# Layer 1's attention: products with V one tile behind, turned maps in two places, next scores biased first

## The chip, the cores and the metric

The kernel runs on one core of one Trainium2 chip. The metric is the device time of one execution in microseconds; given is the median of several runs. The engines are called as in the profile: PE (TensorE), DVE (VectorE), ACT (ScalarE), POOL (GpSimd), SP (SyncE); PEld are TensorE's weight loads.

## What is computed

A decoder trunk of two layers over 1024 tokens of 1024 channels, in float32. Layer 0 has a differential attention and a pooling mixer, layer 1 a gated short convolution and a dilated attention; each is followed by an output projection and a SwiGLU FFN. The change touches layer 1's attention alone, in the reference:

```
for layer in range(DEPTH):
    h = rmsnorm(x, norm_mix[layer])
    ...
        yc = short_conv_gate(bg, cg, hc, od_conv_w[i])
        q = rmsnorm(q.reshape(bsz, seq, D_HEADS, HEAD_DIM), od_q_gain[i])
        k = rmsnorm(k.reshape(bsz, seq, D_HEADS, HEAD_DIM), od_k_gain[i])
        v = v.reshape(bsz, seq, D_HEADS, HEAD_DIM)
        yd = dilated_attention(q, k, v, slopes_d).reshape(bsz, seq, D_WIDTH)
        x = x + jnp.concatenate([yc, yd], axis=-1) @ od_w_out[i]
    x = x + swiglu_ffn(x, norm_ffn[layer], ...)
```

There are 8 heads of 64 channels. The three branches of the dilated attention (a near window, every 4th and every 16th key) come to one softmax over the causal keys, in which a key counts as many times as branches hold it: the kernel adds one table of distances times the head's slope and of logarithms of that count to the scores.

## The kernel before, in words

The kernel is written out by hand, one instruction stream for each engine, with semaphores between them. Every engine runs its own list in order; nothing reorders the work.

**Tiles and units.** Layer 1's attention has 4 units (UNITS) of two heads each, m = 0 and 1, and in each unit 8 tiles (NT) of 128 queries, i = 0 to 7, so 32 tiles n = 8u + i (TILES0). Tile i has 128(i + 1) causal keys. Per tile and head the steps are:
- score (L973): two products of 512 columns at most for each half of the keys, with K1 and K2, into banks 0-1 (m = 0) or 2-3 (m = 1) of PS. It is made two tiles ahead of the rest, and waits (s_mx) for the bias of the tile before, which empties the bank.
- bias (biased, L2058, on DVE): scores plus the table, into PR[m][i % 2], with the row's extreme into NMX.
- expo (L1529, ACT): the exponential in place, with its row sum into DEN.
- turn (L985, PE): i + 1 transposes of PR into one of three banks of PS (4 to 6), taken in turn by turn_bank (L391); for i >= 4 it fills a second bank (c = 1). It waits for expo and for the copy that empties its bank.
- turned: ACT (L1547) copies up to 512 columns to PT[m], DVE (L2170) the columns above 512.
- weigh (L1005, PE): the product of the turned map PT[m] with V, 2(i + 1) PE instructions of 64 columns, into bank 7 (weighed, L394), which both heads share. So it waits for o_ok of the other head, that is, for the scaled output that empties the bank.
- scaled (L2176, DVE): reciprocal of DEN (L2180), then the output times it into Y (L2182).

**Order on TensorE (L1178 to L1199)**, per tile: turn 0, score 0 of tile i + 2, turn 1, weigh 0, score 1 of tile i + 2, weigh 1. **On VectorE (L2167 to L2207)**, per tile: biased 0 of tile i + 1, at i = 6 the next unit's table for head 0 (next_bias, L2051), scaled 1 of tile i - 1, turned 0, biased 1 of tile i + 1, turned 1, scaled 0; at i = 6 the next unit's table for head 1; at i = 7 scaled 1 as well. **On ScalarE (L1636 to L1658)**, per tile: turned 0, expo 0 of the next tile, turned 1, expo 1 of the next tile.

**The next unit's stacks.** Queries and keys of the next unit are split into a high part (ACT, stack_high L1498) and the rest (POOL, low_stack L841, its instruction at L845) while the unit runs: six pieces in a fixed order (STACK, L353), keys 0 and 1, then queries in four pieces. In layer 1 ACT makes pieces 0 and 1 at tiles 1 and 2, piece 2 ahead of turned 0 of tile 6, piece 3 after expo 0 there, piece 4 after expo 1 there, and piece 5 after turned 1 of tile 7. The queries go to the same QST that the unit reads, so they can't be made before its scores are done. PE waits for pieces 2 and 3 ahead of the scores of tile 6, and at the first tile of a unit, ahead of turn 0, for all six:

```
if i == 0:
    pe.wait_ge(stack_lo, following)
```

After the last tile PE turns Y (turn_y, L1132) and begins the output projection, whose weights ACT and DVE split after the last product (L1660, L2210).

Of the kernel before, what the change touches and what calls it, by code (L numbers as in the profile page):

```python
# [82 lines left out]
def trunk(nc, a, out):  # L83
    ctx = ExitStack()
    with ctx:
# [152 lines left out]
        PR = [[at(f"PR{m}{b}", [P, TOK], F32, oHL + 16 * KB + 8 * KB * m + 4 * KB * b) for b in range(2)] for m in range(2)]  # L238
        YJ = at("YJ", [P, P], F32, oK + 4 * KB)
# [684 lines left out]
        def _(pe):  # L924
# [60 lines left out]
            def turn(L, m, g, h, i):  # L985

                if L == 0:
                    if g + i > 0:
                        pe.wait_ge(t_ea[0][0], g + i)
                    pe.wait_ge(c_ok, g + i + 1)  # L990
                else:
                    pe.wait_ge(s_ex[m][L], g + i + 1)
                for c in range(i // 4 + 1):
                    if L == 1 and TURNS.index((m, i, c)) >= 3:
                        m0, i0, c0 = TURNS[TURNS.index((m, i, c)) - 3]
                        if c0 == 0:
                            pe.wait_ge(t_ea[m0][1], g + i0 + 1)
                        else:
                            pe.wait_ge(t_ed[m0][1], h + i0 - 3)
                    for j in range(4 * c, min(4 * c + 4, i + 1)):  # L1000
                        last = pe.transpose(turn_bank(L, m, i, c)[:, P * (j - 4 * c):P * (j - 4 * c) + P],  # L1001
                                            PR[m if L else 1][i % 2][:, P * j:P * j + P], IDN[:])
                last.then_inc(t_pe[m][L], 1)

            def weigh(L, m, u, g, h, i):  # L1005

                pe.wait_ge(t_ea[m][L], g + i + 1)
                if L == 1 and i >= 4:
                    pe.wait_ge(t_ed[m][1], h + i - 3)

                if L == 0:
                    pe.wait_ge(o_ok[0][0], g + i + 2)
                else:
                    pe.wait_ge(o_ok[1 - m][1], g + i + 2 + m)
                w, off = (P, u * P) if L == 0 else (HD, u * P + HD * m)
                for j in range(i + 1):
                    last = pe.matmul(weighed(L, m, i), PT[m if L else i % 2][:, P * j:P * j + P], V[:, j, bass.ds(off, w)],  # L1017
# [12 lines left out]
            for L in range(2):  # L1030
# [117 lines left out]
                if L == 0:  # L1148
                    for u in range(UNITS):
                        b, g = u % 2, NT * u  # L1150
                        following = stacks_before(0, u + 1)
                        for i in range(NT):
# [11 lines left out]
                            if i > 0:  # L1164
                                weigh(0, 0, u, g, 0, i - 1)
                            elif u > 0:
                                weigh(0, 0, u - 1, g - NT, 0, NT - 1)
# [4 lines left out]
                            turn(0, 0, g, 0, i)  # L1172
# [3 lines left out]
                    weigh(0, 0, UNITS - 1, NT * (UNITS - 1), 0, NT - 1)  # L1176
                else:
                    for u in range(UNITS):  # L1178
                        b, g, h = u % 2, NT * u, 4 * u
                        following = stacks_before(1, u + 1)  # L1180
                        for i in range(NT):
# [5 lines left out]
                            turn(1, 0, g, h, i)  # L1187
# [5 lines left out]
                            turn(1, 1, g, h, i)  # L1193
                            weigh(1, 0, u, g, h, i)
# [4 lines left out]
                            weigh(1, 1, u, g, h, i)  # L1199
# [165 lines left out]
        def _(act):  # L1365
# [73 lines left out]
            for L in range(2):  # L1439
# [107 lines left out]
                def turned(m, g, i):  # L1547
# [6 lines left out]
                    else:  # L1554
                        w = min(HALF, P * (i + 1))
                        src, to = turn_bank(1, m, i, 0)[:, 0:w], PT[m]
# [285 lines left out]
        def _(dve):  # L1842
# [93 lines left out]
            for L in range(2):  # L1936
# [229 lines left out]
                else:  # L2166
                    for u in range(UNITS):  # L2167
                        b, g = u % 2, NT * u

                        def turned(m, i):  # L2170
                            if i >= 4:
                                dve.wait_ge(t_pe[m][L], g + i + 3)
                                w = P * (i + 1)
                                v.tensor_copy(PT[m][:, HALF:w], turn_bank(1, m, i, 1)[:, 0:w - HALF]).then_inc(t_ed[m][1], 1)

                        def scaled(m, i):  # L2176

                            c = m + 2 * (i % 2)
                            dve.wait_ge(s_ex[m][1], g + i + 1)
                            att.link(v.reciprocal(RDN[:, c:c + 1], DEN[:, c:c + 1]))  # L2180
                            dve.wait_ge(o_pe[m][1], g + i + 1)
                            v.tensor_scalar(Y[:, i, bass.ds(u * P + HD * m, HD)], weighed(1, m, i), RDN[:, c:c + 1], None,  # L2182
                                            ALU.mult).then_inc(o_ok[m][1], 1)
# [5 lines left out]
                        for i in range(NT):  # L2189
                            if i == NT - 1:  # L2190
                                att.wait()
                            more = u + 1 < UNITS or i + 1 < NT
                            if more:
                                biased(0, b, g, i + 1)
                            if i == NT - 2 and u + 1 < UNITS:
                                next_bias(0)
                            if i > 0:
# [274 lines left out]
```

## Time and profile before

| | us |
|---|---|
| median of 3 runs | 2240.63 (2240.45 to 2242.11) |
| the profiled execution, its own time | 2241.53 |
| its span in the profile | 2239.7 |
| PE busy | 2183.4 (97%) |
| DVE busy | 1256.6 (56%) |
| ACT busy | 878.5 (39%) |
| POOL busy | 790.5 (35%) |
| layer 1's attention in that span | 1350 to 1497 |

Times in rows are microseconds from the start of the span; a row of a timeline gives start, duration, engine, line, operation, output<-inputs, shape and count, and in brackets the engine's idle time before it with what ended it. Starts are recorded and ends of matmuls are modelled, so matmuls that follow each other overlap in the rows, and an idle time is shorter than the gap from start to start. PEclk is the granted TensorE clock as a share of 2.4 GHz.

### The profile page before, as it was taken

Reading aid. Unit: us, or ns where it says so; the run is one execution under the profiler, and the core shown is the slowest. Engines: PE = TensorE matmul, PEld = TensorE weight load, DVE = VectorE, ACT = ScalarE, POOL = GpSimd, SP = SyncE. Lnnn points to the kernel's source line nnn. Section 1 sums busy time; section 2 is a strip of 40 time slices with the busy share of each in tenths; the row PEclk is TensorE's granted clock in tenths of the full one; section 3 lists DMA queues with packets and bytes.
Section 4 is the critical chain, followed back from the end, with each engine's and each line's share of the span. In section 5 each row is a group of like instructions: output and inputs, shape, how many; then the busy total and the mean of one; then the engine's idle time right before and its main releaser. Section 6 shows DMA issues by size and latency. Waiting matters only on the chain.

```text
span 2239.7 us, 29918 instructions
## 1 busy us (share of the span) xinstructions
PE 2183.4 (97%) x10632; PEld 1827.2 (82%) x10632; DVE 1256.6 (56%) x1761; ACT 878.5 (39%) x1433; POOL 790.5 (35%) x533
## 2 busy tenths in 40 slices
PE   8999899999999999999999998999999999999999
PEld 7886798888888887888888877888888888887887
DVE  4245875775555654557322246665775555554555
ACT  4124874443333334444211137652443333334433
POOL 1022542467676662002000032200467676662000
PEclk9999999999999999999999999999999999999999
DMA  5021120055555547674111111101055555547665
GB/s 182 10 78 30 39 86 20 19 179 197 197 188 169 165 158 264 192 242 124 38 45 49 47 57 38 39 20 57 21 177 197 197 188 169 169 161 262 196 190 196
DMA packets 218908, 282.92 MB, mean 126 GB/s; under 512 B 11441, under 2 KB 120497, under 8 KB 218801
## 3 DMA queue, kind: packets, MB, share of 16 engines
q1 hardware_dynamic: 218512, 281.45, 39.1%
q8 instruction: 66, 1.08, 0.2%
q14 instruction: 42, 0.34, 0.1%
q10 hardware_dynamic: 288, 0.05, 0.0%
HBM read 199.67 MB, written 73.40 MB: 122 GB/s over the span
## 4 chain that ended last, share of the span: by engine, by line
PE 72%; issue 12%; DVE 3%; ACT 2%; POOL 1%; DMA 0%; SPq 0%; POOLq 0%; DVEq 0%; ACTq 0%
PE PS L1312 12%; PE PS L1314 12%; PE PS L1313 12%; PE PS L1339 6%; PE PS L1340 6%; PE PS L1341 6%; PE PS L1017 4%; PE PS L927 2%; PE PS L929 2%; PE PS L928 2%; PE PS L1001 2%; PE PS L981 1%; PE PS L982 1%; PE PS L945 1%; POOL QRS L838 1%
## 5 line engine op out<-in xcount | busy, mean ns | idle before, releaser
L1848 DVE TENSOR_TENSOR LINEl<-LINE,HIGH 128x1024 fp32r<-128x1024 f32 x154 | 193.8, 1264 | 170.3 <-ACT HIGH L1370 170.0
L1370 ACT ACTIVATE HIGH<-LINE 128x1024 fp32r<-128x1024 f32 x154 | 162.5, 1059 | 236.7 <-PE PS L1341 234.2
L1339 PE MATMUL PS<-HIGH 128*128 128x512 f32 x616 | 241.4, 392 | 7.0 <-DVE LINEl L1848 7.0
L1340 PE MATMUL PS<-LINEl,HIGH 128*128 128x512 f32 x616 | 241.1, 391 | 0.0
L1341 PE MATMUL PS<-HIGH,LINEl 128*128 128x512 f32 x616 | 241.0, 391 | 0.0
L1848 DVE TENSOR_TENSOR SLOTl<-BLOCKS,RING 128x512 fp32r<-128x512 f32 x168 | 155.1, 923 | 96.6 <-ACT RING L1370 92.1
L807 POOL TENSOR_TENSOR ST<-ST 128x512 f32<-128x512 f32 x132 | 194.5, 1474 | 34.6 <-DMA ST<-in_ffn_w_down 26.0
L1370 ACT ACTIVATE RING<-BLOCKS 128x512 fp32r<-128x512 f32 x168 | 105.9, 631 | 227.7 <-PE PS L1314 219.4
L1848 DVE TENSOR_TENSOR SLOTl<-SLOT,RING 128x512 fp32r<-128x512 f32 x126 | 137.2, 1089 | 85.9 <-ACT RING L1370 85.7
L838 POOL TENSOR_TENSOR QRS<-QMS,EXPO 128x8 f32<-128x8 f32 x32 | 52.0, 1639 | 375.4 <-DVE QMS L2016 375.3
L1339 PEld LDWEIGHTS PS<-HIGH 128*128 128x128 f32 x616 | 116.5, 189 | 32.6 <-DVE LINEl L1848 8.3
L1341 PEld LDWEIGHTS PS<-HIGH,LINEl 128*128 128x128 f32 x616 | 116.5, 189 | 24.2
L1340 PEld LDWEIGHTS PS<-LINEl,HIGH 128*128 128x128 f32 x616 | 116.2, 189 | 24.1
L1312 PE MATMUL PS<-B1h,RING 128*128 128x512 f32 x336 | 130.7, 389 | 0.0
L1313 PE MATMUL PS<-B1l,RING 128*128 128x512 f32 x336 | 130.7, 389 | 0.0
L1314 PE MATMUL PS<-B1h,SLOTl 128*128 128x512 f32 x336 | 130.7, 389 | 0.0
L1370 ACT ACTIVATE RING<-SLOT 128x512 fp32r<-128x512 f32 x126 | 79.2, 630 | 125.2 <-PE PS L1314 114.9
L1017 PE MATMUL PS<-V,PT 128*128 128x64 f32 (+1 forms) x864 | 112.8, 276 | 10.4 <-ACT Y L1370 7.9
L1017 PEld LDWEIGHTS PS<-V,PT 128*128 128x128 f32 x864 | 106.3, 193 | 18.7 <-ACT PT L1370 12.3
L779 POOL TENSOR_TENSOR SLOT<-BLOCKS 128x512 f32<-128x512 f32 x42 | 55.3, 1317 | 187.7 <-DMA BLOCKS<-in_ffn_w_up 187.7
L812 POOL TENSOR_TENSOR RST<-MSQ,EXPO 128x1 f32<-128x1 f32 x32 | 22.9, 718 | 265.8 <-DVE MSQ L1866 265.8
L2069 DVE CUSTOM_DVE_ANT_0 PR<-PS,BIAS 128x256 f32<-128x256 f32 (+7 forms) x128 | 96.3, 755 | 18.9 <-PE PS L1001 8.7
(304 smaller groups left out, 5662.2 us busy)
## 6 DMA issues: line engine op xcount, KB each, us to landing
LINE<-hidden SPq DMA_DIRECT2D x154, 256.0 KB, 2.8
hidden<-HID SPq DMA_DIRECT2D x44, 512.0 KB, 4.5
ST<-in_ffn_w_down SPq DMA_DIRECT2D x44, 512.0 KB, 4.1
sums<-ST SPq DMA_DIRECT2D x22, 1024.0 KB, 6.2
hidden<-ST SPq DMA_DIRECT2D x22, 1024.0 KB, 6.8
LINE<-sums SPq DMA_DIRECT2D x88, 256.0 KB, 3.0
BLOCKS<-in_ffn_w_gate SPq DMA_DIRECT2D x42, 512.0 KB, 4.0
BLOCKS<-in_ffn_w_up SPq DMA_DIRECT2D x42, 512.0 KB, 5.2
```

Of the source, the lines that this page charges most:

```text
L807: nc.gpsimd.tensor_tensor(dst, x, y, op).then_inc(st_sum, 1)
L838: nc.gpsimd.tensor_tensor(QRS[:, 8 * b:8 * b + 8], QMS[:, 8 * b:8 * b + 8], EXPO[:, 0:8], ALU.pow).then_inc(qk_rs, 1)
L1017: last = pe.matmul(weighed(L, m, i), PT[m if L else i % 2][:, P * j:P * j + P], V[:, j, bass.ds(off, w)], start=(j == 0), stop=(j == i))
L1312: pe.matmul(dst, lh, rh[:, k, :], start=k == 0 and not adds_on, stop=False, skip_group_check=adds_on)
L1313: pe.matmul(dst, lh, rl[:, k, :], start=False, stop=False, skip_group_check=adds_on)
L1314: last = pe.matmul(dst, ll, rh[:, k, :], start=False, stop=k == 3, skip_group_check=adds_on)
L1339: pe.matmul(dst, hi[:, 0, ts], hi[:, 1, :], start=j == 0 and not adds_on, stop=False, skip_group_check=adds_on)
L1340: pe.matmul(dst, hi[:, 0, ts], lo[:, 1, :], start=False, stop=False, skip_group_check=adds_on)
L1341: pe.matmul(dst, lo[:, 0, ts], hi[:, 1, :], start=False, stop=j == NJ - 1, skip_group_check=adds_on).then_inc(dn_pe, 1)
L1370: return nc.scalar.activation(dst, src, ACT.Copy, **kw)
L1848: return v.tensor_tensor(dst, src, hi.bitcast(F32), ALU.subtract)
L2069: v.tensor_tensor_reduce(out=PR[m][t % 2][:, 0:keys], in0=PS[:, 1024 * m:1024 * m + keys], in1=table, scale=-1.0, scalar=3.0e38, op0=ALU.a ...
```

## The change

It concerns layer 1's attention, on three engines.
- Storage: a second place for the turned map of each head, PTL[m][1], over the keys' and queries' first rows of QK (unit 0's), free once unit 0's stacks are made. ACT and DVE wait for that (stack_lo) and for the product of two tiles ago (o_pe), in the place of waits that the single buffer did not need.
- PE: per tile turn 0, score 0 of tile i + 2, weigh 0 of the tile before, turn 1, score 1 of tile i + 2, weigh 1 of the tile before; the two products of the last tile stand behind the loop. The bank waits of turn now run on across units.
- DVE: per tile the reciprocal of head 0 of the tile before, biased 0 of the next tile, the reciprocal of head 1, scaled 1 of two tiles ago, biased 1, turned 0, (tile 6: next unit's table for head 0), scaled 0 of the tile before, turned 1, (tile 6: next table for head 1).
- ACT: the place it writes to, and the wait for it. Its order, POOL's and SP's lists are unchanged. Layer 0's calls are rewritten for the new arguments and do the same.

```diff
@@ -236,6 +236,8 @@
         BIAS = [at(f"BIAS{m}", [P, TOK], F32, oHL + 4 * KB * m) for m in range(2)]
         PT = [at(f"PT{m}", [P, TOK], F32, oHL + 8 * KB + 4 * KB * m) for m in range(2)]
         PR = [[at(f"PR{m}{b}", [P, TOK], F32, oHL + 16 * KB + 8 * KB * m + 4 * KB * b) for b in range(2)] for m in range(2)]
+
+        PTL = [[PT[m], at(f"PTB{m}", [P, TOK], F32, oC + 16 * KB * m)] for m in range(2)]
         YJ = at("YJ", [P, P], F32, oK + 4 * KB)
 
         SM = small("SM", 16 + 64)
@@ -982,39 +984,42 @@
                     last = pe.matmul(dst, q, K2[b][m][:, c0:c1], start=False, stop=True)
                 last.then_inc(s_pe[m][L], 1)
 
-            def turn(L, m, g, h, i):
-
+            def turn(L, m, u, i):
+                n = NT * u + i
                 if L == 0:
-                    if g + i > 0:
-                        pe.wait_ge(t_ea[0][0], g + i)
-                    pe.wait_ge(c_ok, g + i + 1)
+                    if n > 0:
+                        pe.wait_ge(t_ea[0][0], n)
+                    pe.wait_ge(c_ok, n + 1)
                 else:
-                    pe.wait_ge(s_ex[m][L], g + i + 1)
+                    pe.wait_ge(s_ex[m][L], n + 1)
                 for c in range(i // 4 + 1):
-                    if L == 1 and TURNS.index((m, i, c)) >= 3:
-                        m0, i0, c0 = TURNS[TURNS.index((m, i, c)) - 3]
+                    if L == 1 and (u > 0 or TURNS.index((m, i, c)) >= 3):
+
+                        u0, k0 = divmod(len(TURNS) * u + TURNS.index((m, i, c)) - 3, len(TURNS))
+                        m0, i0, c0 = TURNS[k0]
                         if c0 == 0:
-                            pe.wait_ge(t_ea[m0][1], g + i0 + 1)
+                            pe.wait_ge(t_ea[m0][1], NT * u0 + i0 + 1)
                         else:
-                            pe.wait_ge(t_ed[m0][1], h + i0 - 3)
+                            pe.wait_ge(t_ed[m0][1], 4 * u0 + i0 - 3)
                     for j in range(4 * c, min(4 * c + 4, i + 1)):
                         last = pe.transpose(turn_bank(L, m, i, c)[:, P * (j - 4 * c):P * (j - 4 * c) + P],
                                             PR[m if L else 1][i % 2][:, P * j:P * j + P], IDN[:])
                 last.then_inc(t_pe[m][L], 1)
 
-            def weigh(L, m, u, g, h, i):
-
-                pe.wait_ge(t_ea[m][L], g + i + 1)
+            def weigh(L, m, n):
+
+                u, i = n // NT, n % NT
+                pe.wait_ge(t_ea[m][L], n + 1)
                 if L == 1 and i >= 4:
-                    pe.wait_ge(t_ed[m][1], h + i - 3)
-
+                    pe.wait_ge(t_ed[m][1], 4 * u + i - 3)
                 if L == 0:
-                    pe.wait_ge(o_ok[0][0], g + i + 2)
+                    pe.wait_ge(o_ok[0][0], n + 2)
                 else:
-                    pe.wait_ge(o_ok[1 - m][1], g + i + 2 + m)
+                    pe.wait_ge(o_ok[1 - m][1], n + 2 + m)
                 w, off = (P, u * P) if L == 0 else (HD, u * P + HD * m)
+                turned = PTL[m][i % 2] if L else PT[i % 2]
                 for j in range(i + 1):
-                    last = pe.matmul(weighed(L, m, i), PT[m if L else i % 2][:, P * j:P * j + P], V[:, j, bass.ds(off, w)],
+                    last = pe.matmul(weighed(L, m, i), turned[:, P * j:P * j + P], V[:, j, off:off + w],
                                      start=(j == 0), stop=(j == i))
                 last.then_inc(o_pe[m][L], 1)
 
...
@@ -1184,19 +1187,24 @@
                                 pe.wait_ge(stack_lo, following)
                             if i == 2 and u == 0:
                                 pe.wait_ge(staged_rest, 128)
-                            turn(1, 0, g, h, i)
+                            turn(1, 0, u, i)
                             if i == NT - 2 and more:
                                 pe.wait_ge(staged[1 - b], 128 + 64 * (u // 2 + b + 1))
                                 pe.wait_ge(stack_lo, following + 3)
                             if more:
                                 score(1, 0, b, g, i + 2)
-                            turn(1, 1, g, h, i)
-                            weigh(1, 0, u, g, h, i)
+
+                            if g + i > 0:
+                                weigh(1, 0, g + i - 1)
+                            turn(1, 1, u, i)
                             if i == NT - 2 and more:
                                 pe.wait_ge(stack_lo, following + 4)
                             if more:
                                 score(1, 1, b, g, i + 2)
-                            weigh(1, 1, u, g, h, i)
+                            if g + i > 0:
+                                weigh(1, 1, g + i - 1)
+                    for m in range(2):
+                        weigh(1, m, TILES0 - 1)
 
                 if L == 0:
                     for k in range(BLOCKS_IN, 4 * NT):
@@ -1553,7 +1561,11 @@
                         src, to = PS[:, 4 * HALF:4 * HALF + w], PT[i % 2]
                     else:
                         w = min(HALF, P * (i + 1))
-                        src, to = turn_bank(1, m, i, 0)[:, 0:w], PT[m]
+                        if g + i >= 2:
+                            act.wait_ge(o_pe[m][1], g + i - 1)
+                        elif i == 1:
+                            act.wait_ge(stack_lo, STACK_AT[1] + len(STACK0))
+                        src, to = turn_bank(1, m, i, 0)[:, 0:w], PTL[m][i % 2]
                     copy(to[:, 0:w], src).then_inc(t_ea[m][L], 1)
 
                 def scaled(n):
@@ -2164,48 +2176,61 @@
                             unit_scaled(u - 1)
                     add_block(BLOCKS_IN - 1)
                 else:
-                    for u in range(UNITS):
-                        b, g = u % 2, NT * u
-
-                        def turned(m, i):
-                            if i >= 4:
-                                dve.wait_ge(t_pe[m][L], g + i + 3)
-                                w = P * (i + 1)
-                                v.tensor_copy(PT[m][:, HALF:w], turn_bank(1, m, i, 1)[:, 0:w - HALF]).then_inc(t_ed[m][1], 1)
-
-                        def scaled(m, i):
-
-                            c = m + 2 * (i % 2)
-                            dve.wait_ge(s_ex[m][1], g + i + 1)
-                            att.link(v.reciprocal(RDN[:, c:c + 1], DEN[:, c:c + 1]))
-                            dve.wait_ge(o_pe[m][1], g + i + 1)
-                            v.tensor_scalar(Y[:, i, bass.ds(u * P + HD * m, HD)], weighed(1, m, i), RDN[:, c:c + 1], None,
-                                            ALU.mult).then_inc(o_ok[m][1], 1)
+                    def turned(m, n):
+                        u, i = n // NT, n % NT
+                        if i >= 4:
+                            dve.wait_ge(t_pe[m][1], n + 3)
+                            dve.wait_ge(o_pe[m][1], n - 1)
+                            dve.wait_ge(stack_lo, STACK_AT[1] + len(STACK0))
+                            w = P * (i + 1)
+                            v.tensor_copy(PTL[m][i % 2][:, HALF:w], turn_bank(1, m, i, 1)[:, 0:w - HALF]).then_inc(t_ed[m][1], 1)
+
+                    def denominator(m, n):
+                        c = m + 2 * (n % 2)
+                        dve.wait_ge(s_ex[m][1], n + 1)
+                        att.did(v.reciprocal(RDN[:, c:c + 1], DEN[:, c:c + 1]))
+
+                    def scaled(m, n):
+                        u, i = n // NT, n % NT
+                        c, off = m + 2 * (n % 2), u * P + HD * m
+                        att.wait()
+                        dve.wait_ge(o_pe[m][1], n + 1)
+                        v.tensor_scalar(Y[:, i, off:off + HD], weighed(1, m, i), RDN[:, c:c + 1], None, ALU.mult).then_inc(o_ok[m][1], 1)
+
+                    for n in range(TILES0):
+                        u, i = n // NT, n % NT
+                        b, g, more = u % 2, NT * u, n + 1 < TILES0
 
                         def next_bias(m):
                             dve.wait_ge(s_mx[m][1], g + 9)
                             bias(m, 1 - b, 2 * u + 2 + m)
 
-                        for i in range(NT):
-                            if i == NT - 1:
-                                att.wait()
-                            more = u + 1 < UNITS or i + 1 < NT
-                            if more:
-                                biased(0, b, g, i + 1)
-                            if i == NT - 2 and u + 1 < UNITS:
-                                next_bias(0)
-                            if i > 0:
-                                scaled(1, i - 1)
-                            turned(0, i)
-                            if more:
-                                biased(1, b, g, i + 1)
-                            turned(1, i)
-                            scaled(0, i)
-                            if i == NT - 2 and u + 1 < UNITS:
-                                next_bias(1)
-                            if i == NT - 1:
-                                scaled(1, i)
-
+
+                        if n > 0:
+                            denominator(0, n - 1)
+                        if i == NT - 1:
+                            att.wait()
+                        if more:
+                            biased(0, b, g, i + 1)
+                        if n > 0:
+                            denominator(1, n - 1)
+                        if n > 1:
+                            scaled(1, n - 2)
+                        if more:
+                            biased(1, b, g, i + 1)
+                        turned(0, n)
+                        if i == NT - 2 and u + 1 < UNITS:
+                            next_bias(0)
+                        if n > 0:
+                            scaled(0, n - 1)
+                        turned(1, n)
+                        if i == NT - 2 and u + 1 < UNITS:
+                            next_bias(1)
+                    denominator(0, TILES0 - 1)
+                    scaled(1, TILES0 - 2)
+                    scaled(0, TILES0 - 1)
+                    denominator(1, TILES0 - 1)
+                    scaled(1, TILES0 - 1)
 
                 def split_o(g):
                     dve.wait_ge(wo_hi, WO_AT[1] + g + 1)
```

## Rows read from the trace of the kernel before

**Rows 1.** Busy time by stretch, second unit: us, PE, PEld, DVE, ACT, POOL busy, PEclk, DMA

```profile
1389.40:1425.00 35.60, 34.11 (x267) 31.29 (x266) 23.12 (x74) 24.52 (x54) 9.83 (x6) 1.00 0.13 31
```

**Rows 2.** PE's waits in the attention: us in total, times, longest

```profile
PE PS L981 <- DVE NMX L2069: 2.1, 3, 0.7
PE PS L1017 <- DVE Y L2182: 1.8, 5, 0.5
```

**Rows 3.** Timeline of PE, second unit's tiles 6 and 7, next unit's tile 0

```profile
1412.78 0.94 PE L1001 MATMUL PS<-IDN,PR 128*128 128x128 f32 x7
...
1413.73 1.23 PE L1001 MATMUL PS<-IDN,PR 128*128 128x128 f32 x7
1414.79 1.67 PE L1017 MATMUL PS<-V,PT 128*128 128x64 f32 x14
1416.77 0.33 PE L981 MATMUL PS<-K,QST 128*128 128x128 f32 x1 [0.30 <-POOL QST L845]
...
1419.73 1.26 PE L1001 MATMUL PS<-IDN,PR 128*128 128x128 f32 x8
1420.83 1.90 PE L1017 MATMUL PS<-V,PT 128*128 128x64 f32 x16
...
1422.73 0.28 PE L982 MATMUL PS<-K,QST 128*128 128x256 f32 x1
1423.26 1.97 PE L1017 MATMUL PS<-V,PT 128*128 128x64 f32 x16 [0.25 <-DVE Y L2182]
1425.07 0.28 PE L1001 MATMUL PS<-IDN,PR 128*128 128x128 f32 x1
1426.06 0.44 PE L981 MATMUL PS<-K,QST 128*128 128x384 f32 x1 [0.71 <-DVE NMX L2069]
...
1427.02 0.33 PE L982 MATMUL PS<-K,QST 128*128 128x384 f32 x1
1427.51 0.41 PE L1017 MATMUL PS<-V,PT 128*128 128x64 f32 x2
```

**Rows 4.** Timeline of ACT, same stretch

```profile
1413.75 0.60 ACT L1370 ACTIVATE PT<-PS 128x512 f32<-128x512 f32 x1 [2.41 <-PE PS L1001]
...
1421.03 0.60 ACT L1370 ACTIVATE PT<-PS 128x512 f32<-128x512 f32 x1 [0.36 <-PE PS L1001]
1421.65 0.84 ACT L1370 ACTIVATE QST<-QK 64x768 fp32r<-64x768 f32 x1
```

**Rows 5.** Timeline of POOL, same stretch

```profile
1415.99 0.72 POOL L845 TENSOR_TENSOR QST<-QK,QST 64x256 fp32r<-64x256 f32 x1 [3.84 <-ACT QST L1370]
...
1422.57 1.81 POOL L845 TENSOR_TENSOR QST<-QK,QST 64x768 fp32r<-64x768 f32 x1 [2.14 <-ACT QST L1370]
```

**Rows 6.** Timeline of DVE, same unit

```profile
1408.17 1.08 DVE L2069 CUSTOM_DVE_ANT_0 PR<-PS,BIAS 128x896 f32<-128x896 f32 x1
...
1416.78 1.28 DVE L2051 SCALAR_TENSOR_TENSOR BIAS<-DIST,SM,MASK 128x1024 f32<-128x1024 f32 x1
...
1422.84 0.28 DVE L2182 TENSOR_SCALAR Y<-PS,RDN 128x64 f32<-128x64 f32 x1 [1.05 <-PE PS L1017]
...
1425.35 0.28 DVE L2182 TENSOR_SCALAR Y<-PS,RDN 128x64 f32<-128x64 f32 x1 [2.16 <-PE PS L1017]
```

**Rows 7.** Timeline of PE, end of the last unit

```profile
1485.99 1.67 PE L1017 MATMUL PS<-V,PT 128*128 128x64 f32 x14
1488.21 1.75 PE L1017 MATMUL PS<-V,PT 128*128 128x64 f32 x14 [0.55 <-DVE Y L2182]
...
1496.97 3.60 PE L1145 MATMUL PS<-IDN,Y 128*128 128x128 f32 x16 [0.54 <-DVE Y L2182]
```

**Rows 8.** Busy time and granted clock by stretch, columns as in rows 1

```profile
1492.00:1496.50 4.50, 3.88 (x34) 3.64 (x32) 1.12 (x4) 2.49 (x3) 0.00 (x0) 1.00 0.00 0
1496.50:1501.00 4.50, 3.60 (x16) 3.27 (x16) 4.46 (x4) 3.33 (x3) 0.00 (x0) 0.62 0.01 2
1421.00:1425.00 4.00, 3.75 (x34) 3.58 (x34) 1.11 (x4) 1.93 (x4) 1.81 (x1) 1.00 0.02 4
```

More of the change, by code:

```diff
@@ L1162, in _ @@
                                 score(0, 0, b, g, i + 2)
-                            if i > 0:
-                                weigh(0, 0, u, g, 0, i - 1)
-                            elif u > 0:
-                                weigh(0, 0, u - 1, g - NT, 0, NT - 1)
+                            if g + i > 0:
+                                weigh(0, 0, g + i - 1)
                             if more:
@@ L1171, in _ @@
                                 turn_y(0)
-                            turn(0, 0, g, 0, i)
+                            turn(0, 0, u, i)
                             if g + i >= FILL_FROM:
@@ L1175, in _ @@
                     turn_y(1)
-                    weigh(0, 0, UNITS - 1, NT * (UNITS - 1), 0, NT - 1)
+                    weigh(0, 0, TILES0 - 1)
                 else:
                     for u in range(UNITS):
-                        b, g, h = u % 2, NT * u, 4 * u
+                        b, g = u % 2, NT * u
                         following = stacks_before(1, u + 1)
@@ L1198, in _ @@
                                 score(1, 1, b, g, i + 2)
-                            weigh(1, 1, u, g, h, i)
+                            if g + i > 0:
+                                weigh(1, 1, g + i - 1)
+                    for m in range(2):
+                        weigh(1, m, TILES0 - 1)
                 if L == 0:
@@ L2187, in next_bias @@
                             bias(m, 1 - b, 2 * u + 2 + m)
-                        for i in range(NT):
-                            if i == NT - 1:
-                                att.wait()
-                            more = u + 1 < UNITS or i + 1 < NT
-                            if more:
-                                biased(0, b, g, i + 1)
-                            if i == NT - 2 and u + 1 < UNITS:
-                                next_bias(0)
-                            if i > 0:
-                                scaled(1, i - 1)
-                            turned(0, i)
-                            if more:
-                                biased(1, b, g, i + 1)
-                            turned(1, i)
-                            scaled(0, i)
-                            if i == NT - 2 and u + 1 < UNITS:
-                                next_bias(1)
-                            if i == NT - 1:
-                                scaled(1, i)
+                        if n > 0:
[23 more added lines that the diff above has]
+                    scaled(1, TILES0 - 1)
                 def split_o(g):
```

## The prediction

> **What bounds it now.** I read the kernel by stretch first, then the waits, then TensorE's timeline, then what ACT, POOL and VectorE do around each wait. In layer 1's attention one unit of two heads takes 35.6 us and PE is busy 34.1 of them [rows 1]: TensorE is the bound, and only the time between its instructions can be won. The list of waits shows 2.1 us for VectorE's score maxima and 1.8 for scaled outputs [rows 2]; GpSimd's query stack comes next. Since the ends of matmuls are modelled, a wait shows whole only from start to start. In a full stream a product with V starts every 0.11 us (16 in 1.81 us, from 1423.26 to 1425.07), and a transpose too (7 in 0.69, less an overlap of 0.08 with the score behind) [rows 3]. What lies above that at tiles 6, 7, 0 and 1 of a unit:
> - the second map's turn at tile 6 takes 1.06 us for 0.77, at tile 7 1.10 for 0.88: it waits for ACT's copy, for its bank; 0.29 and 0.22 lost
> - second score at tile 6, behind GpSimd: 1.98 us after the start of 14 products worth 1.56; 0.42, with its restart 0.5
> - second product at tile 7: 0.53 us after a score half worth 0.12; 0.41 lost
> - first score at tile 0: 0.99 after one transpose of 0.11; 0.88. VectorE scales the last output (1425.35) [rows 6] before it biases the next scores, which this one waits for
> - second product at tile 0: 0.49 behind a half worth 0.18; 0.31. Tile 1 has the same wait, with a score longer by 0.12 ahead of it: 0.2.
>
> In the last unit these waits are longer, as no score lies between. From 1485.99 to 1496.97, 10.98 us, it makes 60 products (6.7) and 16 transposes (1.75) [rows 7]: 2.5 lost, of which the last 0.7, ahead of layer 1's output turns, stays; with tile 6's bank wait just before it (estimate 0.4, as tile 7's), 2.2 can go. All this is some 10 us of 2240: that is the ceiling.
>
> **The change, part by part.** No instruction of work is added or taken away; a few waits on semaphores, copies into a second place and the order change. Per tile TensorE now does turn 0, score 0, product 0 of the tile before, turn 1, score 1, product 1 of the tile before.
>
> *Waits that go.* At three unit starts: 0.88 (the bias now stands ahead of the scaled output on VectorE), 0.31 and 0.2, so 1.4 x 3 = 4.2. A product of a whole tile now lies between the two turns, so the bank waits go, and turn 1 and score 1 lie between the two products, some 1.1 us at tile 7, so that wait goes: (0.29 + 0.22 + 0.41) x 3 = 2.8. Unit 0's start runs at the half clock and gives away four products there: 0.5. In the last unit the 2.2 us go. Gone in all: 9.7.
>
> *Waits that come.* The two products still share one bank, so each waits for the scaled output of the other. Product end to VectorE's start is 0.28 us (1425.07 to 1425.35) [rows 3, 6]; from that start to the next product 0.42 (1422.84 to 1423.26) [rows 3, 6]: 0.70 in all. At tile 0 turn and score are 0.11 + 0.38 = 0.49 us, so the second product is 0.2 late, x3 = 0.6. At tile 2 VectorE has its two biases, two reciprocals and two outputs within about 2 us of TensorE's work at tile 1; bounds 0 and 0.3, I take 0.15 (what a full VectorE leaves over), x4 = 0.6. In the last unit the two products of tile 31 have nothing between: 0.7 x 2 = 1.4.
>
> *The query stacks of the next unit* are the main term. ACT copies piece 5 after its copy of the second turned map of tile 7, GpSimd then makes the low part, and TensorE's first turn of the next unit waits for that. From the end of turn 1 (1420.83) ACT starts 0.20 later, the stack copy at 1421.65 (0.84 us), GpSimd at 1422.57 for 1.81: ready at 1424.43 with 0.05 of release, 3.60 after the turn [rows 3 to 5]. Now it is covered by 4.24 us of TensorE (1420.83 to 1425.07) [rows 3]. After the change product 0 stands ahead of turn 1, so behind it only score 1 (0.25) and the product of tile 6 (14 x 0.112 = 1.56) are left: 1.81 of cover for 3.60. New wait 1.8 us at each of three unit starts: 5.4. Piece 3 at tile 6 has the same shape: ACT's chain starts at the end of turn 0 (copy 1413.75, exponential, stack copy, GpSimd 1415.99 for 0.72) [rows 4, 5] and frees score 1 at 3.99 us into the tile, as now (1412.78 to 1416.77) [rows 3]. TensorE is there at 3.1 (0.69 + 0.26 + 12 x 0.112 + 0.77), since its product is shorter and the bank wait gone: 0.9 to 1.0 lost in place of 0.5, +0.5 x 3 = 1.5. The next unit's bias (1.28 us, 1416.78) [rows 6] now stands ahead of a scaled output at tile 6; this output would be free for its product at 3.8 us, the stack frees the score at 4.0 and its two halves end at 4.3: nothing, while the stack is late; without that cover 0.4 x 3.
>
> Come in all: 0.6 + 0.6 + 1.4 + 5.4 + 1.5 = 9.5. Against 9.7, the order alone is worth -0.2 us. ACT has copies, exponentials and a key stack at tile 1, more than TensorE's new 1.8 us there (2 x (0.22 + 0.48 + 0.22)), but enters that tile early, since tile 0 now takes 4.5 with the products of tile 7: nothing.
>
> **The clock.** From 1492.0 to 1496.5 TensorE ran at the full 2.4 GHz with 34 instructions, almost all V products; in the next 4.5 us the mean is 0.62, that is 3.4 us at the half level of 1.2 GHz, and 16 transposes take 3.6 us, about 0.22 each [rows 7, 8]. What it did before the fall: V products, with idle times of 0.54 us [rows 7]. Between 1421 and 1425 V products with one wait of 0.25 kept the full clock [rows 3, 8]. A unit start with 1.8 us of idle between 14 products and 16 is emptier than the stretch before that fall. So I expect a fall at most of the three. In 3.4 us at 0.22 instead of 0.11 some 15 instructions are lost, 1.7 us; bounds 0 and 1.7, I take 1.5 as small waits run within it: 4.5.
>
> The Trainium skill (TensorE: Matmul & The Clock Gate, "Why this matters for your kernels") has the clock stay up unless PE idles for a long gap between bursts of matmuls. By that rule waits of this length cost no clock and the sum stays at -0.2; the fall after idle times of 0.54 [rows 7, 8] speaks against it.
>
> **Sum.** The profiled execution took 2241.5; 2241.5 - 0.2 + 4.5 = 2245.8; the median of the runs is 0.9 lower: 2244.9. A measurement of this kernel tells about 0.2% (4.5 us) from no change; the forecast lies inside, at the upper edge.
>
> **Rivals.**
> 1. The clock holds at the unit starts, the products on both sides of the wait being enough for it. For: the stretch at 1421 held with a small wait [rows 8]. 2241.5 - 0.2 - 0.9 = 2240.4. Chance 0.2. The rule of the Trainium skill above would give the same.
> 2. The stack is not the bound at unit starts: ACT or GpSimd would have to be 1.8 us earlier. For: GpSimd is idle 2.1 us before this piece [rows 5]. Against: that idle time is ACT's, and ACT's is TensorE's own turn [rows 4]. Then 5.4 go, 0.2 at tile 0 comes back three times, and the clock holds: 2240.4 - 5.4 + 0.6 = 2235.6, faster. Chance 0.08.
> 3. Slower. VectorE becomes late: an output of head 0 now stands behind the other head's bias and the copy of the turned map. At tile 5 this is 0.28 (latency) + 0.28 (the other output) + 1.08 (bias of 896 columns) [rows 6] + 0.4 at most for a copy of 256 columns (estimate from that row) = 2.0 us into the tile, while the product it serves ends at 0.66 + 0.94 + 10 x 0.112 = 2.7 (score of 1024 keys estimated as four halves, each 0.18 x 512/384), so 0.7 is spare. It decides once bias and copy together exceed TensorE's turn, score and product; if every tile from 2 to 5 then waits 0.2, that is 16 x 0.2 = 3.2: 2248.1. Chance 0.17.
> That two buffers free nothing, since the outputs still share a bank, is part of the sum: the last unit's 0.7.
>
> **Chances.** Forecast with falls at two or three starts: 0.55, of which 0.33 stays within 0.2% (three full falls of 1.7 reach 2245.5). With the cases above: faster 0.08, same 0.53, slower 0.39. Low end: no falls, tile 2 free: 2239.8. High end between the forecast and rival 3: 2247.5. Its own range is 2243 to 2246.
>
> **What would show it.** Right: TensorE's waits list GpSimd's query stack with 5 to 7 us in six waits (recorded idle is less than from start to start), the longest some 1.6, three of them before the first transpose of a unit; the wait for maxima at unit starts gone; bank waits gone; mean clock of the attention below before's, with two or three falls to half; the units after the first 37 us, last unit shorter. Wrong: POOL before the first turn with under 1 us (the chain), full clock throughout (the clock term), or new waits for scaled outputs at tiles 2 to 5 (rival 3).

## The result, and the profile after

The changed kernel takes 2250.1 us (median of 8 runs, 2245.4 to 2256.7) where the kernel before took 2241.0 (8 runs, 2240.4 to 2242.9): ratio 1.0036, with a 95% interval from 1.0026 to 1.0047. It is slower by 9.1 us, and it scatters over 11 us where the kernel before scatters over 2.5. The profiled execution is the slowest of the eight: 2256.7 us, span 2254.6. So its rows show more loss than the median has.

The list of TensorE's waits of the changed kernel, over layer 1's attention (in total, times, longest; PTB in the rows is the second place for a turned map):

```profile
PE PS L1005 <- POOL QST L847: 5.0, 3, 1.7
PE PS L983 <- POOL QST L847: 1.4, 3, 0.5
PE PS L1022 <- DVE Y L2198: 1.1, 2, 0.5
...
PE PS L1150 <- DVE Y L2198: 0.5, 1, 0.5
```

The waits for the maxima and for ACT's copies of [rows 2, 3] are gone, those for scaled outputs are left in the last unit alone. In their place stands the query stack: three times ahead of a unit's first turn (L1005), three times ahead of the second score of tile 6 (L983). TensorE's timeline of the changed kernel at the first unit's end, as [rows 3] one unit later (start, duration):

```profile
1372.53 0.94 PE L1005 MATMUL PS<-IDN,PR 128*128 128x128 f32 x7
...
1375.16 0.93 PE L1005 MATMUL PS<-IDN,PR 128*128 128x128 f32 x7
1376.57 0.33 PE L983 MATMUL PS<-K,QST 128*128 128x128 f32 x1 [0.47 <-POOL QST L847]
...
1379.30 1.67 PE L1022 MATMUL PS<-V,PT 128*128 128x64 f32 x14
1380.80 1.05 PE L1005 MATMUL PS<-IDN,PR 128*128 128x128 f32 x8
...
1381.92 1.67 PE L1022 MATMUL PS<-V,PT 128*128 128x64 f32 x14
1385.28 0.33 PE L1005 MATMUL PS<-IDN,PR 128*128 128x128 f32 x1 [1.68 <-POOL QST L847]
1385.36 0.42 PE L983 MATMUL PS<-K,QST 128*128 128x384 f32 x1
...
1385.80 3.35 PE L1022 MATMUL PS<-V,PTB 128*128 128x64 f32 x16
1388.94 0.42 PE L1005 MATMUL PS<-IDN,PR 128*128 128x128 f32 x1
```

and ACT's and GpSimd's share of the chain:

```profile
1381.88 0.60 ACT L1378 ACTIVATE PTB<-PS 128x512 f32<-128x512 f32 x1 [1.65 <-PE PS L1005]
1382.51 0.84 ACT L1378 ACTIVATE QST<-QK 64x768 fp32r<-64x768 f32 x1
```

```profile
1383.42 1.80 POOL L847 TENSOR_TENSOR QST<-QK,QST 64x768 fp32r<-64x768 f32 x1 [2.80 <-ACT QST L1378]
```

From the end of turn 1 (8 transposes from 1380.80, so 1381.68) to the next unit's first turn (1385.28) are 3.60 us, as foretold. 14 products from 1381.92 should have ended at 1383.48: 1.8 us lost. The second score of tile 6 starts at 4.04 us into the tile (3.99 foretold), 0.64 us behind the end of its transposes (1375.16 + 0.77), where the sum has 0.9 to 1.0. The rest of that term stands at the first score, for which the sum has none: it starts 1.05 us into the tile (1372.53 to 1373.58) where it started at 0.69, and 0.10 behind the end of GpSimd's part of piece 2 (1372.75 + 0.73).

The 16 products of tile 7 behind the wait then take 3.14 us (1385.80 to 1388.94) where they took 1.81. Busy time and granted clock of the changed kernel behind each unit's start, and at the end (us, PE, PEld, DVE, ACT, POOL busy, PEclk, DMA share, GB/s):

```profile
1384.00:1399.00 15.00, 13.72 (x72) 13.01 (x73) 5.06 (x23) 6.11 (x18) 2.82 (x2) 0.66 0.00 1
1424.00:1439.00 15.00, 13.92 (x74) 13.09 (x75) 4.99 (x23) 6.51 (x18) 3.39 (x2) 0.66 0.00 1
1460.00:1478.00 18.00, 16.32 (x85) 15.44 (x85) 5.76 (x25) 6.07 (x18) 2.00 (x2) 0.62 0.00 1
1500.00:1520.00 20.00, 17.45 (x87) 15.57 (x86) 9.83 (x14) 9.31 (x9) 0.00 (x0) 0.66 0.15 52
```

A mean of 0.66 over 15 us is 10.2 us at the half level of 1.2 GHz, 0.62 over 18 is 13.7, 0.66 over 20 is 13.6: 48 us in four falls in this slowest execution, where [rows 8] had one of 3.4. Behind the first start the clock still stands at full level for some 0.7 us: it falls at about 1385.95, TensorE having started again at 1385.28. The last fall comes between the products of tile 31, where three waits of 0.54 us follow each other:

```profile
1503.05 1.97 PE L1022 MATMUL PS<-V,PTB 128*128 128x64 f32 x16 [0.54 <-DVE Y L2198]
1505.56 3.65 PE L1022 MATMUL PS<-V,PTB 128*128 128x64 f32 x16 [0.54 <-DVE Y L2198]
1509.74 3.65 PE L1150 MATMUL PS<-IDN,Y 128*128 128x128 f32 x16 [0.54 <-DVE Y L2198]
```

It reaches into the output projection, whose products then start 0.43 us apart (0.23 in the kernel before, from 1502.32 on):

```profile
1514.32 0.77 PE L929 MATMUL PS<-WOh,HH 128*128 128x512 f32 x1 [0.93 <-DVE WOl L1860]
1514.88 0.63 PE L930 MATMUL PS<-WOl,HH 128*128 128x512 f32 x1
1515.31 0.63 PE L931 MATMUL PS<-WOh,HL 128*128 128x512 f32 x1
```

The scatter of the runs is the clock's too: those with a mean granted clock of 0.989 took 2245.4, 2246.2 and 2247.2 us, those of 0.985 took 2252.1 and 2256.7.

### The profile page after: what moved, and what is told of

Read it like the earlier page. It is cut to its first block, busy times and chain, and to the rows that moved or that the text cites. A ratio compares the mean times of both kernels' runs of the same rounds, so it can differ in the third digit from the quotient of the medians.

```text
span 2254.6 us, 30018 instructions
## 1 busy us (share of the span) xinstructions
PE 2194.7 (97%) x10632; PEld 1840.8 (82%) x10632; DVE 1257.0 (56%) x1761; ACT 879.3 (39%) x1433; POOL 791.3 (35%) x533
## 4 chain that ended last, share of the span: by engine, by line
PE 73%; issue 19%; DVE 3%; ACT 2%; POOL 2%; DMA 1%; SPq 0%; POOLq 0%; DVEq 0%; ACTq 0%
PE PS L1320 12%; PE PS L1322 12%; PE PS L1321 12%; PE PS L1347 6%; PE PS L1349 6%; PE PS L1348 6%; PE PS L1022 4%; PE PS L929 3%; PE PS L931 3%; PE PS L930 3%; PE PS L1005 2%; PE PS L983 1%; POOL QRS L840 1%; PE PS L984 1%; PE PS L947 1%
## 5 line engine op out<-in xcount | busy, mean ns | idle before, releaser
L929 PE MATMUL PS<-HH,WGh 128*128 128x512 f32 x256 | 99.8, 390 | 2.2 <-ACT V L1378 2.2
L929 PE MATMUL PS<-WQh,HH 128*128 128x512 f32 x256 | 101.8, 398 | 0.0
```

Of the source, the lines that this page charges most:

```text
L929: pe.matmul(dst, lh, rh, start=first, stop=False)
```

## Experiments

Theory A: the late piece of the query stack makes TensorE wait, and the clock falls behind that wait; both together are the loss. Its rivals: the new order on TensorE (B), the new order on VectorE (C), or the wait without the clock. Each run was timed beside the kernel before on the same chip, 2241.6 to 2242.8 us there. The changed kernel itself was timed beside 2241.0 alone, so where two runs from different chips are compared, up to 1.8 us can be the chips'; beside its own neighbour the changed kernel is at +9.1 us.

**1. Piece 5 early.** Piece 5 needs only that the unit's scores are done, which they are at tile 6:

```diff
+                        if i == NT - 1:
+                            following(5)
                         turned(0, g, i)
...
                         turned(1, g, i)
-                        if i == NT - 1:
-                            following(5)
```

> The changed kernel with one step moved: ACT makes the next unit's query piece 5 ahead of its first copy of tile 7 instead of after its second. Theory A (the late piece makes TensorE wait 1.85 us at each of three unit starts, and the clock falls there): the three waits ahead of the first turn of a unit go, no stretch at half clock at the unit starts, time 2236 to 2240 us (a fall near the last unit's end may stay, up to 4 us). Rival B (the new order itself, with tile 7's products moved into tile 0, is what lets the clock fall, or costs time between the engines): half clock at unit starts stays, time 2246 us or more.

Measured: 2235.3 us, ratio 0.9970 (0.9958 to 0.9981), 0.7 below the range of A and 10.7 below B's. TensorE's waits in it, over the attention, and the clock at the places of the changed kernel's falls:

```profile
PE PS L983 <- POOL QST L847: 1.4, 3, 0.5
...
PE PS L1022 <- DVE Y L2198: 1.1, 2, 0.5
```

```profile
1384.00:1399.00 15.00, 14.93 (x116) 13.71 (x117) 8.71 (x35) 11.32 (x28) 4.76 (x2) 1.00 0.05 10
1424.00:1439.00 15.00, 15.00 (x116) 14.11 (x116) 10.46 (x37) 12.57 (x27) 4.77 (x2) 1.00 0.29 72
1460.00:1478.00 18.00, 18.00 (x146) 17.12 (x144) 13.01 (x41) 12.66 (x26) 0.00 (x0) 1.00 0.01 2
```

The L1005 row for GpSimd is gone, in each of these stretches the clock is 1.00, and TensorE makes 116 matmuls in the first 15 us where the changed kernel made 72. One moved line takes 14.8 us off (15.7 beside the neighbours): B falls as the main cause. One fall is left, at the last unit's end: 0.84 over the 22 us to 1500, that is 7 us at the half level.

**2. Piece 3 early as well**, `following(2, 3)` ahead of the first copy of tile 6 and the later `following(3)` gone.

> As the run with piece 5 early, and piece 3 made together with piece 2 ahead of ACT's first copy of tile 6. Theory A: TensorE's wait for the second score of tile 6 (start to start 0.64 us over) goes at three units too, so 1.5 to 2.5 us less than with piece 5 alone; then the table of the next unit, which stands ahead of a scaled output on VectorE, shows as a wait of about 0.4 us at tile 6. 2234 to 2238 us. Rival B: no gain over the run with piece 5 alone.

Measured: 2234.1 us, 0.9965 (0.9951 to 0.9979), 1.2 less than with piece 5 alone, where 1.5 to 2.5 were expected; the intervals overlap. No wait for GpSimd is listed any more, but the first score of tile 6 still starts 1.04 us into the tile (1373.76 to 1374.80), again 0.10 behind GpSimd's part of piece 2 (1373.97 + 0.73). The second product of tile 6 waits for its output instead, as foretold: its start comes 0.40 us after the score's second half, worth 0.11, and 0.43 after VectorE starts on that output (1377.19), behind the table.

```profile
1377.22 0.28 PE L984 MATMUL PS<-K,QST 128*128 128x128 f32 x1
1377.62 1.52 PE L1022 MATMUL PS<-V,PTB 128*128 128x64 f32 x12
```

**3. The wait filled with transposes that nobody reads**, pieces late as in the changed kernel:

```diff
                             if i == 0:
+                                if u > 0:
+                                    pe.wait_ge(t_ed[0][1], 4 * u)
+                                    for _ in range(15):
+                                        pe.transpose(bank(4)[:, 0:P], IDN[:], IDN[:])
                                 pe.wait_ge(stack_lo, following)
```

> The changed kernel with 15 transposes of the identity added on TensorE at each of three unit starts, ahead of the wait for the query pieces, into a bank that is free there; the wait for the pieces itself ends when it did. Theory A1 (most of the loss is clock, not wait): full clock through the unit starts, 2241 to 2244 us, wait for pieces down to under 0.3 us as recorded though TensorE does no useful work more. Rival A2 (the wait itself is the loss): no change from the changed kernel, 2249 to 2251 us.

Measured: 2240.2 us, 0.9993 (0.9984 to 1.0002). The wait is as long as before, 15 transposes stand in it, and the clock holds:

```profile
1385.78 1.81 PE L1190 MATMUL PS<-IDN 128*128 128x128 f32 x15
1387.65 0.33 PE L1005 MATMUL PS<-IDN,PR 128*128 128x128 f32 x1
...
1388.16 1.89 PE L1022 MATMUL PS<-V,PTB 128*128 128x64 f32 x16
1389.89 0.28 PE L1005 MATMUL PS<-IDN,PR 128*128 128x128 f32 x1
```

```profile
1384.00:1399.00 15.00, 14.87 (x120) 13.52 (x119) 7.67 (x32) 9.59 (x25) 4.21 (x2) 1.00 0.00 1
1424.00:1439.00 15.00, 14.93 (x117) 13.64 (x117) 8.71 (x34) 11.42 (x28) 4.77 (x2) 1.00 0.07 14
1460.00:1478.00 18.00, 17.93 (x138) 16.38 (x137) 11.63 (x43) 11.67 (x29) 0.00 (x0) 1.00 0.01 1
```

What is left is one fall of 3.4 us in the output projection (0.91 over the 20 us to 1520), behind a wait of 2.6 us for its weights; at the last unit's end, where the three waits of 0.54 us stand as before, it is 1.00. This splits the loss: 9.9 us are the clock (2250.1 to 2240.2; 10.8 beside the neighbours), 4.9 the waits themselves (2240.2 to 2235.3, on one chip, where 1.8 x 3 stood in the sum). The price of the fall behind the first start: from the unit's first turn to the third tile's 11.0 us in the changed kernel (1385.28 to 1396.28) and 6.65 here (1387.65 to 1394.30): 4.35.

**4. Two starts filled, the last unit's left bare.**

> The run with filler transposes, but only at the second and third unit's starts; the last unit's start has the bare wait. The all-filled kernel gave 2240.2, the changed kernel 2250.1. If each start costs the same through the clock, 2243 to 2244 us, with the clock at half for about 10 us after that one start. If falls feed each other (a fall at one start moves or lengthens the later ones), 2241 to 2242 us or over 2245.

Measured: 2244.2 us, 1.0014 (1.0004 to 1.0024), runs from 2241.4 to 2250.8. One bare start costs 4.0 us more than none, near the 3 to 4 expected, or 3.2 beside the neighbours; over three that is 12 or 9.6, against 9.9 or 10.8 measured. The scatter is back with one bare wait. Profiled (2243.3 us), the fall behind it lasted 6.8 us (0.81 over 18), not the 10 expected.

**5. The last unit's end filled** with 5 such transposes ahead of each of the two last products and of the turns of Y, pieces late.

> The changed kernel with 5 transposes of the identity into a free bank in each of the three waits of 0.7 us at the last unit's end (ahead of the two last products and of the turns of Y); pieces late as in the changed kernel. Theory A says that most of the clock's loss stands at the unit starts: 2246 to 2249 us, and no fall that reaches into the output projection. If the end of the last unit is where the long falls cost most: 2243 to 2245 us.

Measured: 2246.6 us, 1.0025 (1.0016 to 1.0034), 3.5 less than the changed kernel (4.1 beside the neighbours). The two intervals overlap, so that the last unit's end costs some 3.5 is likely, not shown. Granted clock in the profiled run: 0.66 behind the first start, 1.00 behind the second, 0.72 behind the third, 1.00 at the end and in the output projection. TensorE's recorded wait is 1.68 or 1.69 us at all three starts; so not every such wait is followed by a fall.

**6. The wait in the kernel before.** Its order is kept; ACT makes two copies into unread rows ahead of piece 5:

```diff
                         if i == NT - 1:
+                            if u + 1 < UNITS:
+                                for row in (0, UNITS):
+                                    copy(QK[:, row, :], V[:, 0:2, :].rearrange("p t c -> p (t c)"))
                             following(5)
```

> The kernel before with its order kept and piece 5 made late: ACT makes two copies of 128x1024 into rows that nobody reads (about 1.05 us each) ahead of it at three units' ends. By the chain there was 0.7 us of cover left, so TensorE waits some 1.4 us at each of three unit starts. Theory A (a wait there costs its length and a stretch at half clock of about 10 us, whatever the order of the products): falls at most of the three unit starts, 3 x 1.4 for the waits and 2 to 4 us for each fall, 2249 to 2256 us. Rival B (the clock falls because of the new order): full clock at unit starts and 2245 to 2247 us.

Measured: 2246.6 us, 1.0024 (1.0013 to 1.0036), below the range of A and within B's. The wait is there:

```profile
PE PS L1001 <- POOL QST L845: 3.2, 3, 1.1
```

and behind two of the three starts the clock fell, but for a short time:

```profile
1384.00:1399.00 15.00, 13.52 (x91) 11.73 (x89) 7.23 (x31) 11.20 (x29) 4.53 (x3) 0.89 0.00 1
1424.00:1439.00 15.00, 13.50 (x100) 11.81 (x98) 8.32 (x34) 12.37 (x30) 6.55 (x3) 1.00 0.01 1
1460.00:1478.00 18.00, 16.65 (x113) 14.86 (x113) 9.64 (x39) 11.34 (x30) 1.80 (x1) 0.91 0.00 1
```

0.89 over 15 us is 3.3 at half level, 0.91 over 18 is 3.2. So the falls need no new order, which speaks for A, though they are a third of the 10 us that it has. That a wait stands there does not yet give the length of the fall. In the old order small tiles follow the wait, with scores of up to 1024 columns soon after; in the new one 32 products of 64 columns with V. The waits differ as well (1.1 and 1.7 recorded), so which of the two makes the falls three or four times as long stays open.

**7. VectorE's part alone**, on the kernel before: the last scaled output of a unit moves behind the next tile's bias for head 0 (`elif u > 0: last(1, NT - 1)` behind `biased(0, ...)`, in place of `if i == NT - 1: scaled(1, i)`).

> The kernel before with one part of the change alone: at a unit's end VectorE puts the last scaled output behind the next tile's bias for head 0, not ahead of it. TensorE's order, storage and ACT's order as before. Theory A: the wait for the maxima at three unit starts (0.88 us each by the starts) goes, and the product behind waits for the scaled output a little longer: 2239 to 2240.5 us, full clock at unit starts. Rival C (the changed kernel's loss comes in part from VectorE's new order): 2243 us or more.

Measured: 2239.6 us, 0.9985 (0.9976 to 0.9994): 3.2 us gained, where the three waits of 0.88 give 2.6. C falls: in the old order this part is a gain.

**8. and 9. Early pieces in the old order**, alone and with part 7.

> The kernel before with pieces 3 and 5 made early by ACT, and nothing else of the change. Theory A: only the wait of the second score at tile 6 goes (0.5 us at three units), 2239 to 2240.5 us: most of what early pieces give the changed kernel is its own new wait. Rival B: more than 3 us gained here as well, which would make the pieces a bound of both kernels.

> The same with the query pieces 3 and 5 made early by ACT. The early pieces alone gave 2244.2, with a fall of the clock at one unit start where waits for VectorE's scaled output had grown. If the wait for the maxima was what let the clock fall there, this comes out at 2237 to 2239 us at full clock; if not, at 2241 us or more. Either way slower than the changed order with early pieces (2234.1), since the bank waits and the last unit's waits stay.

Measured: 2244.2 (1.0010, 1.0001 to 1.0019) and 2240.9 (0.9992, 0.9984 to 1.0001): neither is in a range that was expected, and neither gains by the pieces (the second is 1.3 above run 7). In the first the wait for GpSimd is gone, but waits for scaled outputs rose from 1.8 us in 5 to 2.8 in 8, and the clock fell at one unit start for 3.3 us (0.89 over 15):

```profile
PE PS L1017 <- DVE Y L2180: 2.8, 8, 0.5
PE PS L981 <- DVE NMX L2067: 2.1, 3, 0.7
```

So in the old order the wait only changes its place. That fall explains at most 1.7 of 2.3 us; the rest is open.

**10. Turns together again**: `turn(1, 1, u, i)` ahead of `weigh(1, 0, ...)`, the rest as changed.

> The changed kernel with turn 1 ahead of product 0 again (turn 0, score 0, turn 1, product 0 of the tile before, score 1, product 1 of the tile before), the pieces made where they were. Theory A (the wait at a unit start is 3.6 us of chain from the end of turn 1, less what TensorE has behind it): product 0 of tile 6, 1.56 us, covers the chain again, so the wait falls from 1.85 to about 0.3 us, the bank waits of 0.2 to 0.3 us at tiles 6 and 7 come back, the clock holds: 2236 to 2240 us. Rival B (lagging products let the clock fall): 2245 us or more.

Measured: 2243.8 us, 1.0003 (0.9994 to 1.0012), runs from 2238.9 to 2247.9, between the ranges of A and B. The chain is covered again: no wait for the stack stands at a unit start, and the first turn follows 14 products after their 1.58 us.

```profile
1383.95 1.75 PE L1022 MATMUL PS<-V,PT 128*128 128x64 f32 x14 [0.25 <-DVE Y L2198]
1385.53 0.28 PE L1005 MATMUL PS<-IDN,PR 128*128 128x128 f32 x1
```

So the cover of the chain is as the sum has it. The time is not: only a score is left between the two products, so seven waits for outputs come to 2.9 us, and the profiled run, the slowest of the eleven, lost clock for 3.4 us at the end of tile 6 in the second unit, behind a wait of 0.57 for the stack (0.93 over the 25 us to 1424), and for 17 us at the last unit's end (0.84 over the 22 us to 1500, 0.75 over the next 20).

**11. and 12. Filling on top of both early pieces.** First the last unit's end, as in 5; then also 42 transposes in the wait for the copies of K ahead of the first scores.

> The changed kernel with pieces 3 and 5 early and the same three waits filled. With the early pieces alone one fall of 6.8 us stood at the last unit's end. If it is due to these waits it goes or moves behind the turns of Y: 2231 to 2233 us; if it stays, 2234 to 2235 us.

> As the run before, and 42 transposes of the identity (4.6 us at full clock) in TensorE's wait of 5.1 us for the copies of K ahead of layer 1's first scores, where every run shows 10 to 14 us at half clock that reach into the first unit. If that fall follows from the empty wait, the first tiles run at full clock: 3 to 5 us less than the run before, 2227 to 2230 us; if not, no change.

Measured: 2233.3 (0.9965, 0.9951 to 0.9979) and 2235.7 (0.9971, 0.9961 to 0.9981). The first loses its fall at the end (clock 1.00 from 1478 to 1520 against 0.84 to 1500 without), but is within the scatter of the 2234.1 of run 2. Part of the gain is taken back behind it: TensorE's wait for the output projection's split weights (L929, VectorE) is 2.6 us there, 0.9 in run 2. The second is 2.4 slower than the first instead of 3 to 5 faster: the transposes themselves ran in part at half clock, and the first turn came at 1353.55 in place of 1352.06. But the clock came back while they ran: 0.53 from 1344.5 to 1348.0, 0.98 from 1348.0 to 1350.75, with nothing but transposes on TensorE in either stretch. It fell again for 3.4 us within the first tiles, and once more at the wait of 2.6 us ahead of the output projection.

The best version without idle work is the changed kernel with both pieces early: 2234.1 us, 7.8 less than the kernel before beside it and 16 less than the change as made.

## Why the prediction was wrong

**What held.** The waits that should go went. The chain of the query stack, the main term, came out at 3.60 us for 3.60 and the waits at 1.8 for 1.8; tile 6 at 4.04 for 3.99, with its loss split over both scores. The last unit's two products wait 0.54 us as recorded. Of the order alone the sum said -0.2 us; with the clock held by filling it is 2240.2 against 2241.9 beside it, -1.7. VectorE never became late at tiles 2 to 5 (rival 3): no such wait is in the list. The stack was the bound (rival 2 falls), and the clock did not hold (rival 1 falls); the rule of the Trainium skill (TensorE: Matmul & The Clock Gate, "Why this matters for your kernels") had it hold through gaps this short. The runs speak against that here: the clock fell behind all three waits of 1.7 us of the changed kernel, behind two of three in run 5, and behind two of three of 1.1 us in run 6.

**What failed** is one term: "In 3.4 us at 0.22 instead of 0.11 some 15 instructions are lost, 1.7 us; bounds 0 and 1.7, I take 1.5 as small waits run within it: 4.5." The place, the cause and the number of falls were right, their size was not. It was taken from the one fall at the attention's end, 3.4 us. Behind the unit starts of the changed kernel's profiled execution a fall lasts 10.2 to 13.7 us, and the first costs 4.35; filling these waits gave back 9.9 us where the term had 4.5. The trace of before had such a fall too, ahead of this attention: the clock is at half from 1346.8 to 1357.0. I took the nearer row for both bounds, when the longer one should have been in the range; 10.2 us at half would have made it 5 per fall and 15 in all, and the range would have reached 2256. As it stands even its high end, 2247.5, is below the 2250.1 measured, and the units after the first take 39.8 us, not 37, in the profiled execution.

A second omission is the last unit's end. There three waits of 0.7 us now follow each other, as the sum has them, but the sum charged only their length. The fall there lasts 13.6 us in the profiled execution, partly in the output projection, which the prediction did not look at, where the kernel before has 3.4. Run 5 puts it at some 3.5 us, not clear of the scatter of the two kernels. This can't be added to the 9.9: with the starts filled (run 3) the same three waits stand at the end and no fall follows them, only one of 3.4 us behind the projection's own wait. Why is open.

With 9.9 in place of 4.5 the sum gives 2250.3, for 2250.1 measured. That says less than it seems to: the 9.9 is itself the measured time less that of run 3, so the agreement is only that of the rest of the sum, 2240.4, with run 3's 2240.2. What makes a fall of 10 us out of one of 3 no run shows.

## What to carry to other kernels

When an order is changed on one engine, follow every chain that starts at a moved instruction to the end on the other engines: here four steps of 3.6 us lost their cover because a product was put ahead of the turn from which they start, and one line on ACT, whose inputs were long ready, gave it back. On TensorE a new wait among small matmuls is to be priced at its length plus a chance of a stretch at half clock, and the range should reach at least to the longest such stretch in the trace. Even that is no upper bound: the trace of before has one of 10.2 us, the changed kernel one of 13.7, run 10 one of 17. Where runs of one kernel scatter far more than those of another, look at the granted clock of each first.

## What the hardware showed that I had not expected

Idle transposes cost nothing in a wait at full clock and held the clock: 45 of them took the changed kernel from 2250.1 to 2240.2 us. They also brought it back from the half level by themselves (run 12). The same kernel without them scatters over 11 us; falls behind like waits can stay away (run 5: one start of three without a fall). And falls differ in length behind like waits: 10.2, 10.2 and 13.7 us in the changed kernel, 6.8 in run 4, all ahead of tile 7's products with V, and 3.4 twice in run 6, ahead of small tiles with their scores.
